# A chunked hybrid block on one core: the delta rule's finished rows turned into columns by a transposing DMA instead of TensorE

## The reference, cut to what matters

```python
proj = rmsnorm(h) @ w_in                       # [T, 3080]: xb, gb, q, k, v, z, b, a
y_lru = rmsnorm(rglru(xb, gb))                 # 512 columns
o = delta_rule(q, k, v, beta, g)               # 4 heads of 128, chunkwise
y_dn = rmsnorm(o, out_norm) * silu(z)          # 512 columns: the "finished rows"
h = h + concatenate([y_lru, y_dn]) @ w_out     # w_out: 1024 x 1024
u2 = rmsnorm(h); logits = u2 @ router          # top group, top two experts of it
h = h + mixture(u2); out = rmsnorm(h)[16:]
```

## Time and profile before

| what | value |
|---|---|
| median of 3 runs | 3208.5 us (3205.51 to 3211.61) |
| the profiled execution's own time | 3197.16 us |
| its span, first to last instruction | 3195.5 us |
| mean granted TensorE clock | 0.969 of full speed |
| busy over the span | PE 92%, DVE 80%, ACT 62%, POOL 28% |
| the mixer's steps | about 270 to 2245 us |
| the experts, then the last norm | about 2245 to 3090, then to the end |

### The profile page before, as it was taken

How to read it: one execution, slowest core, us unless ns; L and a number is a source line. 1 busy time by engine, 2 the same in 40 slices (tenths; PEclk the granted TensorE clock), 3 DMA queues, 4 the chain that set the end, 5 groups by cost and what they waited for, 6 DMA issues and landing times. The chain is left out here.

```text
span 3195.5 us, 81737 instructions
## 1 busy us (share of the span) xinstructions
PE 2935.7 (92%) x28640; PEld 2195.9 (69%) x28641; DVE 2554.9 (80%) x7201; ACT 1973.5 (62%) x4385; POOL 907.7 (28%) x962
## 2 busy tenths in 40 slices
PE   4788999999999999999999999996799999999960
PEld 4777888788878887888788888874344555554530
DVE  6887888888878887888788878876788888888844
ACT  7554666565656566656555565653677777777746
POOL 4422222122212222221222122212344444444420
PEclk9999999999999999999999999998899999999985
DMA  6111232322222222222222222225487877777749
GB/s 231 65 37 32 70 100 72 86 71 75 74 87 68 81 74 81 68 81 76 79 74 74 82 73 80 70 72 211 119 275 223 239 211 199 193 222 217 230 99 394
DMA packets 186113, 396.53 MB, mean 124 GB/s; under 512 B 86992, under 2 KB 86992, under 8 KB 173520
## 3 DMA queue, kind: packets, MB, share of 16 engines
q1 hardware_dynamic: 148896, 286.22, 26.6%
q0 software_dynamic: 29216, 89.30, 12.2%
q10 hardware_dynamic: 7696, 16.86, 1.4%
HBM read 280.05 MB, written 96.01 MB: 118 GB/s over the span
## 5 line engine op out<-in xcount | busy, mean ns | idle before, releaser
L621 PE MATMUL pj<-uT,W 128*128 128x128 f16 x15744 | 974.4, 220 | 12.3 <-POOL W L1939 12.3
L621 PEld LDWEIGHTS pj<-uT,W 128*128 128x128 f16 x15744 | 927.0, 98 | 40.7 <-issue 30.4
L2295 DVE SCALAR_TENSOR_TENSOR W<-W,ecol 128x512 f16<-128x512 f16 x664 | 447.4, 746 | 111.0 <-ACT W L2239 103.1
L2239 ACT ACTIVATE W<-W,ecol 128x512 f16 x664 | 415.8, 708 | 79.2 <-issue 77.0
L2203 PE MATMUL bA<-W,uT 128*128 128x512 f16 x1992 | 447.1, 381 | 5.6 <-issue 4.4
L2203 PEld LDWEIGHTS bA<-W,uT 128*128 128x128 f16 x1992 | 193.6, 98 | 229.1 <-issue 10.0
L2187 PE MATMUL pj<-W,qs 128*128 x664 | 299.8, 594 | 0.9 <-ACT qs L2266 0.9
L2000 POOL TENSOR_TENSOR decb<-upto,nbeta 128x512 f32<-128x512 f16 x33 | 36.1, 1093 | 889.7 <-DVE nbeta L1735 889.7
L1025 ACT ACTIVATE ht<-ht 128x512 f32<-128x512 f32 x256 | 159.2, 623 | 95.2 <-DMA ht<-w_up 89.9
L2187 PEld LDWEIGHTS pj<-W,qs 128*128 128x128 f32 x664 | 119.9, 190 | 120.8 <-issue 120.2
L1055 ACT ACTIVATE qh<-bA 128x256 f32<-128x256 f32 x198 | 76.8, 388 | 191.4 <-PE bA L787 187.7
(11 more groups left out here) (508 smaller groups left out, 6119.8 us busy)
## 6 DMA issues: line engine op xcount, KB each, us to landing
ht<-w_gate SPq DMA_DIRECT2D x128, 256.0 KB, 3.1
ht<-w_up SPq DMA_DIRECT2D x128, 256.0 KB, 3.2
W<-w_gate SPq DMA_DIRECT2D x32, 1024.0 KB
W<-w_up SPq DMA_DIRECT2D x32, 1024.0 KB
W<-w_down SPq DMA_DIRECT2D x32, 1024.0 KB
x_in<-xm SPq DMA_DIRECT2D x33, 512.0 KB, 4.5
ht<-xm SPq DMA_DIRECT2D x32, 512.0 KB, 3.8
h_rows<-ht SPq DMA_DIRECT2D x32, 512.0 KB
```

Source lines behind the costliest of these rows:

```text
L621: mm = pe.matmul(pj[g % 2][:, j, :], w16[:, k, w_half(w_high, COL[GROUPS[g]], 512, j * P, P)], (ul if low_u else uh)[:, k, :], start=(k == ...
L2239: nc.scalar.activation(part_of(wx[par][:, 0], k), raw[:, k], ACT.Copy, scale=ecol[par][:, k:k + 1]).then_inc(sem("wx_high"), 1)
L2295: a = nc.vector.scalar_tensor_tensor(out=part_of(wx[par][:, 1], k), in0=raw[:, k], scalar=ecol[par][:, k:k + 1], in1=part_of(wx[par][:, 0] ...
```

## The change

TensorE's transposes go, in both places where `turn_delta` was called. ScalarE and VectorE keep their places in the order, but read `yt` itself and write the halves as rows, in fp16, into `ks`, whose keys are used up by then. A new function of SyncE, `delta_columns`, waits for `yd_ready` and turns both halves, 128x1024 in fp16, from `ks` to `yt` by one DMA. It stands in `raw_chunks` ahead of piece 2 of the first expert, or, in steps without pieces, behind `raw_chunks`. The matmuls with `w_out` wait for that DMA (`yd_full`, 16 for a transfer). VectorE waits for it too before the convolution overwrites `ks`. Two waits of TensorE for `yd_ready`, which kept bank `bT` for the halves, go or become `kd_ready`.

```diff
+        yd_rows = ks[:].rearrange("p j n -> p (j n)").bitcast(F16)
...
                         for c in range(KT):
                             if c == KT - 2 and n == 1:
                                 turned_rows(s)
+                            if c == 2 and n == 0:
+                                delta_columns(s)
                             if c > 1 or n:
                                 need(sp, sem("w_sq"), s.squares + KT * n + c - 1)
...
+                def delta_columns(s):
+
+                    if s.O:
+                        need(sp, sem("yd_ready"), s.nO)
+                        sp.dma_start(yd16.rearrange("p s j n -> p (s j) n"), yd_rows, transpose=True).then_inc(sem("yd_full"), 16)
...
                     raw_chunks(s)
+                    if not s.sums:
+                        delta_columns(s)
...
                         if j == 4:
-                            need(pe, sem("yd_ready"), s.nO)
+                            need(pe, sem("yd_full"), 16 * s.nO)
...
-                    need(pe, sem("yd_ready"), s.nO)
                     pe.matmul(bTf[:, 0:NE], tri16[:], ohs[:], start=True, stop=True)
...
-                def turn_delta(s):
-
-                    need(pe, sem("yt_ready"), s.nO)
-                    need(pe, sem("kd_ready"), s.nG)
-                    for h in range(H):
-                        mm = pe.transpose(bT[:, h, :], yt[:, h, :], ident[:])
-                    mm.then_inc(sem("yd_full"), 1)
...
                     level_x(s, 3)
-                    if s.O and s.G:
-                        turn_delta(s)
                     project(s, 2, 2)
...
-                        turn_delta(s)
                     late_part(s, 2)
                     if s.G:
                         need(pe, sem("X_new"), 6 * s.pG + 5)
-                        need(pe, sem("yd_ready"), s.nO)
+                        need(pe, sem("kd_ready"), s.nG)
...
                     if s.O:
-                        need(act, sem("yd_full"), s.nO)
-                        nc.scalar.activation(yd16[:, 0], bT[:], ACT.Copy).then_inc(sem("yd_high"), 1)
+                        need(act, sem("yt_ready"), s.nO)
+                        nc.scalar.activation(yd_rows[:, 0:512], flat(yt), ACT.Copy).then_inc(sem("yd_high"), 1)
...
-                    nc.vector.tensor_tensor(yd16[:, 1], bT[:], yd16[:, 0], ALU.subtract).then_inc(sem("yd_ready"), 1)
+                    nc.vector.tensor_tensor(yd_rows[:, 512:1024], flat(yt), yd_rows[:, 0:512], ALU.subtract).then_inc(sem("yd_ready"), 1)
...
+                    if s.P:
+                        need(dve, sem("yd_full"), 16 * s.nO)
                     conv(s, 2, ks, 0, 1, 2, 3)
```

## The result

| | this kernel | before, measured beside it |
|---|---|---|
| median, us | 3225.92 (3220.79 to 3234.3, 9 runs) | 3207.48 (3202.27 to 3213.24, 9 runs) |
| ratio | 1.0061, 95% interval 1.0051 to 1.0072 | |
| profiled execution, span | 3221.1 us | 3195.5 us |

What follows compares the result with a forecast made beforehand. A chain through VectorE and ScalarE, not TensorE (92% busy), was taken to bound the full steps from `level_x` 3 to 5. 0 + 4.8 + 1.6 + 11.0 + 1.6 = +19.0 us on 3208.5 gave 3227.5, own range 3218 to 3236.

Steps and rivals of the forecast that it cites:

- Full steps: TensorE's four transposes, 0.44 us a step, gain 0; TensorE waits 0.73 us instead of 0.29 ahead of `level_x` 5.
- the cover: Chain through VectorE and ScalarE from `level_x` 3 to `level_x` 5; without it, a gain of 13.6 us.
- The DMA in full steps: Lands near 1243.3, 5.1 us before VectorE's wait ahead of the keys' convolution at 1248.43; costs 0.
- Step 4: Step with 16 pieces: piece 2 comes behind `yd_ready`, +4.8 us; TensorE stands 5.0 us, +1.6 for the clock.
- The clock's term: In step 4, 1.6 us lost to a slower TensorE clock after its stall; bounds 0 and twice the 1.6.
- Steps 32 and 33: Expert loads 7.1 us later hold the `h_rows` store, delaying `second_norm` and `w_out` part 4: +11.0 us, clock +1.6.
- The page on queues: Steps 32 and 33: ring order holds the `h_rows` store behind the loads, 11.0 us; by completion order alone 2.3.
- The page on the clock: Advises against idle gaps of a few microseconds: both stalls cost clock, the full steps' 0.73 us waits cost nothing.
- A: Rival: TensorE is the bound at `level_x` 5, each full step gains 0.44 us; 3213.9 us, chance 0.13.
- B: Rival: the tail is cheap, the store of `h_rows` lands in time, +2.3 us there; 3217.2 us, chance 0.13.
- C: Rival: columns land over 8.4 us after `yd_ready` in every step, VectorE waits; 3257 us, chance 0.05.
- D: Rival: unseen slack takes in both special places, the change makes no difference; 3208.5 us, chance 0.05.

Runs made afterwards that it cites:

- experiment 1: Changed kernel with TensorE's transposes put back in steps 4, 32 and 33, so the DMA serves full steps only; 3204.67 us, ratio 1.0 to before.
- experiment 2: Changed kernel with ScalarE's square of weight piece 1 moved behind its copy `qh` for `level_x` 5; 3224.28 us, ratio 1.0053 to before.
- experiment 3: Kernel before, with the same move of ScalarE's square behind its copy `qh`; 3208.21 us, ratio 1.0007.
- experiment 5: Changed kernel with step 4's transposing DMA issued ahead of weight piece 4 instead of piece 2; 3218.65 us in one execution.
- experiment 4: Changed kernel with the twelve loads of the first four experts issued one step later, at the end of step 33; 3236.45 us, ratio 1.0108 to before.
- experiment 9: Changed kernel with the store of `h_rows` in step 33 issued by ScalarE's queue instead of SyncE's; 3229.19 us, ratio 1.0072 to before.
- experiment 6: Experiment 1 plus experiment 2's move of the square, and VectorE takes level 6 in ahead of the queries' last four taps; 3187.81 us, ratio 0.9943 to before.
- experiment 7: Kernel before, with experiment 6's two moves (ScalarE's square, VectorE's level 6) and no transposing DMA; 3195.51 us, ratio 0.9967.
- experiment 8: As experiment 6, but instead of VectorE's move GpSimd's two sums of squares wait for level 6; 3186.29 us, ratio 0.9932 to before.

## Why the prediction was right, step by step

- **Full steps, 0.** Right, and for the reason given; experiment 1 shows it (1.0, 0.9991 to 1.0009). Two details were off. "Waits 0.73 us instead of 0.29" ahead of `level_x` 5 came as 0.18 ahead of `level_y` 4 and 0.51 ahead of `level_x` 5, 0.69 in all: VectorE's turn of X was next in line before ScalarE's copy was. The wait named in step 17 is the same in all of steps 5 to 31 (0.29 to 0.30 us before, 0.51 or 0.52 after). And the cover reaches further than "from `level_x` 3 to `level_x` 5", "Then it runs on": it has a second stretch up to level 7 (experiments 2 and 3), which the prediction did not see and did not need, as the first stretch alone covers the transposes.
- **The DMA in full steps, 0.** Right. Landing takes 3.1 us as the form for `uT` had it, and VectorE does not wait for it.
- **Step 4, +4.8 and +1.6.** 6.05 us against 6.4, with errors against each other. "TensorE takes all of it and stands 5.0 us": it stood 5.74, as ScalarE got piece 2 3.75 us after its issue (420.13 to 423.88), not 3.1, and as it had stood 0.35 us there before (the weight load's wait; the 0.17 us of the prediction are the matmul's). But I left out that TensorE's later wait of 1.45 us at `level_x` 6 would be taken in, and the 0.44 us of transposes: net 4.2 us, not 4.8. The clock's term came as 1.85 by the account of experiment 5, against 1.6. That the sum came within 0.4 us is luck in part.
- **Steps 32 and 33, +11.0 and +1.6.** 14.5 us against 12.6. Each link is there: the loads 7.3 us later (7.1), `second_norm` at 2236.03, which on the clock of before is 2227.5 (2225.9), part 4 at 2242.60, so 2234.0 (2232.5). The term that was mis-sized is the store's landing: I shifted 2218.8 by the 7.1 us, and it came 1.6 later than that. The loads took 35.0 us from the first issue to their last packet instead of 33.9, and VectorE went on 0.4 us behind the store's last packet (2218.92 before, 2235.60 after). Behind it all went as worked out, 2.6 us to land `u_rows` (2236.81 to 2239.43) and 3.2 for the columns. TensorE stood 12.9 us, and the first two groups of six large matmuls of part 4 took 2.72 and 1.93 us instead of 1.45, so 1.75 us lost against 1.6.
- **The page on queues.** By the Trainium skill's "DMA: Bandwidth & Descriptors", section "Queues, rings and completion order", a DMA engine takes a ring's descriptors in order. The packets of the changed kernel agree: the store's first moves 10.5 us after its issue, when the loads run out. So do experiments 4 and 9: without the loads ahead `second_norm` doesn't wait at all, and on another queue the wait for the store ends after 9.3 us instead of 14.6. The 9.3 us that stay are not order within SyncE's queue: the engines move 400 GB/s and more meanwhile. On this the same page of the Trainium skill, section "Issuing engines are not separate DMA queues", says that another issuing engine saves only its own issuing time. Here it saved 5.3 us of the store's wait, so the trace agrees as to the shared engines and goes beyond it as to the queue.
- **The page on the clock.** The page "TensorE: Matmul & The Clock Gate" of the Trainium skill, section "Why this matters for your kernels", warns of gaps of a few microseconds. The windows behind both stalls show 0.50; the full steps, with 0.2 to 0.5 us of wait, show no such loss in experiment 1 (the granted clock is 1.00 from 300 to 2000). The traces agree. The stall of 2.88 us in experiment 5 lies between: the windows from 426 to 436 show 1.00.
- **The rivals.** A (TensorE is the bound) fell by experiment 1; it comes half true only when the chain is shortened at both ends (0.22 of 0.44 us, experiments 6 and 7). B (cheap tail) fell by the 10.36 us. C (late columns) fell by the 3.1 us. D (slack) fell: what slack there was lay in the full steps.
- **The total.** 20.5 us by steps in the profiled executions, 18.4 between the medians, 19.0 predicted. By steps the sum missed by -0.35 us in step 4 and +1.9 in steps 32 and 33, and the interval (16.4 to 23.1) is wider than that, so the agreement to 0.6 us is finer than the sum deserves. Between the two profiled executions the whole difference is 25.6 us; the opening and the experts, which vary by 6 and 16 us between executions, account for 5.9 of it. The forecast's own range, 3218 to 3236, does not follow from the bounds that the prediction names: these give 3215.6 (no loss by the clock, 2.3 us at the tail) to 3233.9 (twice the clock's 3.2 us, 14.2 at the tail).

## What to carry to other kernels

Work taken from the busiest engine pays only where the wait behind it is not someone else's: a wait of 0.3 us that recurs in every period is enough to swallow it all, and to free the time it may take more than one end of the covering chain: here ScalarE's alone gave nothing, ScalarE's with VectorE's gave half of it. A DMA put into an ordered queue is paid for in the steps that are unlike the others: ask, in the first, the last and the doubly loaded steps, what now stands behind its wait, and how many bytes are ahead of the next small transfer that someone waits for. Moving a bulk load later to clear one such transfer puts it ahead of the next.

## What I had not expected of the hardware

- VectorE's convolution taps get slower beside GpSimd's element-wise work. Eight taps of the same shape take 2.31 us where GpSimd runs nothing beside them:

```profile
1240.46 2.31 DVE L1338 SCALAR_TENSOR_TENSOR xc<-ext_xb,cvw,xc 128x128 f32<-128x128 f32 x8
```

The eight of `qs` overlap with GpSimd's operations, and the more they do the longer they take (medians over steps 6 to 31):

| profiled execution | overlap with GpSimd, us | eight taps, us |
|---|---|---|
| experiment 8 | 2.06 | 3.77 |
| after | 2.74 | 3.96 |
| experiment 3 | 3.06 | 4.28 |
| experiment 2 | 3.29 | 4.51 |

That is why starting them sooner changed nothing: 0.55 us sooner is 0.55 us more beside the operation of L2041. Against experiment 2, experiment 8 moves GpSimd's two sums and, in the full steps, nothing else. The page "SBUF — State Buffer" of the Trainium skill, section "Who interferes with whom", says that a VectorE instruction with two SBUF inputs contends with a GpSimd instruction that reads SBUF; the taps have two such inputs (`ext_q` and `qs`), so the runs agree with it, though none of them shows the port itself.
- A store of 512 KB, of the size that for `u_rows` lands in 2.6 us, was waited for until 14.6 us after its issue behind twelve loads of 1 MB in its queue, 9.3 us in another queue beside them, and 26.65 us when issued sooner behind them (experiment 4: 2241.85 to 2268.50). Another queue took it out of the order, and it still shared the bandwidth.
- A stall of TensorE of 5.74 us cost 1.85 us more by the clock, one of 12.9 us 1.75, and one of 2.88 us nothing that shows.
